# The order of the last two tiles in the expert stage: down products of the second to last tile, and low-part gate and up products of the last

## What is computed

```python
h = jax.nn.silu(jnp.einsum('nd,edf->nef', t, w_gate)) * jnp.einsum('nd,edf->nef', t, w_up)
h = h * gate[:, :, None].astype(h.dtype)
return jnp.einsum('nef,efd->nd', h, w_down).reshape(B, T, D)
...
x = _layernorm(DEEPNORM_ALPHA * x + _moe(x, ...), ln2_g, ln2_b)
```

## Time and profile before

| | |
|---|---|
| time, median of 3 runs | 1675.98 us (1675.69 to 1679.21) |
| profiled execution, its own time | 1673.25 us |
| its span, first to last instruction | 1671.6 us |
| mean granted clock of PE | 0.972 |
| PE busy | 1564.2 us (94%) |
| DVE busy | 846.0 us (51%) |
| ACT busy | 663.7 us (40%) |
| POOL busy | 233.2 us (14%) |

### The profile page before, as it was taken

The page is one execution under the profiler, slowest core; times in us unless marked ns, Lnnn a source line. Parts: engine busy times, 40 slices in busy tenths (PEclk is TensorE's granted clock), DMA queues, the critical chain, the costliest instruction groups (busy, mean ns, idle before and its releaser), DMA issues. The chain is left out here.

```text
span 1671.6 us, 25671 instructions
## 1 busy us (share of the span) xinstructions
PE 1564.2 (94%) x9815; PEld 1425.3 (85%) x9815; DVE 846.0 (51%) x1426; ACT 663.7 (40%) x1117; POOL 233.2 (14%) x292
## 2 busy tenths in 40 slices
PE   7999999999999998999999999999997599999980
PEld 7999899889988787899999999999786488888860
DVE  4433463454035654512132232334647799999986
ACT  5422241222245655522121111113112488888866
POOL 1000120013002111130000000000000253333320
PEclk9999999999999999999999999999998699999995
DMA  6111232125211122070344114113433799999736
GB/s 186 41 39 39 76 109 51 39 67 170 79 45 54 63 66 60 30 248 14 139 123 145 43 38 145 38 39 114 141 116 110 269 263 285 325 303 290 193 61 235
DMA packets 154225, 204.34 MB, mean 122 GB/s; under 512 B 14723, under 2 KB 121235, under 8 KB 154104
## 3 DMA queue, kind: packets, MB, share of 16 engines
q1 hardware_dynamic: 135224, 140.82, 26.8%
q0 software_dynamic: 18880, 61.89, 13.1%
HBM read 152.34 MB, written 50.34 MB: 121 GB/s over the span
## 5 line engine op out<-in xcount | busy, mean ns | idle before, releaser
L380 PE MATMUL ps<-xh,slab_hi 128*128 128x384 f32 (+1 forms) x504 | 170.3, 338 | 1.5 <-DVE slab_lo L733 1.5
L380 PE MATMUL ps<-xh,slab_lo 128*128 128x384 f32 (+1 forms) x504 | 165.3, 328 | 0.0
L380 PE MATMUL ps<-xl,slab_hi 128*128 128x384 f32 (+1 forms) x504 | 164.9, 327 | 0.0
L1896 PE MATMUL ps<-xh,slab_lo 128*128 128x384 f32 (+1 forms) x384 | 125.2, 326 | 0.0
L1896 PE MATMUL ps<-xh,slab_hi 128*128 128x384 f32 (+1 forms) x384 | 125.1, 326 | 0.0
L1896 PE MATMUL ps<-xl,slab_hi 128*128 128x384 f32 (+1 forms) x384 | 125.1, 326 | 0.0
L2097 DVE TENSOR_TENSOR gt_sg<-ps,gt_sg 128x384 f32<-128x384 f32 (+1 forms) x48 | 25.7, 536 | 187.3 <-PE ps L1896 187.2
L380 PEld LDWEIGHTS ps<-xh,slab_hi 128*128 128x128 f32 x504 | 95.1, 189 | 11.6 <-issue 9.8
L2866 PE MATMUL ps<-mo_hi_gu,mo_xh 128*128 128x512 f32 x256 | 100.3, 397 | 0.9 <-ACT mo_xh L2969 0.7
L2866 PE MATMUL ps<-mo_hi_gu,mo_xl 128*128 128x512 f32 x256 | 99.0, 391 | 0.0
L2037 ACT ACTIVATE gt_sg<-ps 128x384 f32<-128x384 f32 (+1 forms) x48 | 22.8, 474 | 191.9 <-PE ps L1896 191.9
(11 more groups left out here) (498 smaller groups left out, 4164.5 us busy)
## 6 DMA issues: line engine op xcount, KB each, us to landing
slab_raw<-in_w_in SPq DMA_DIRECT2D x60, 512.0 KB, 4.3
mo_raw_g<-in_w_e_gate SPq DMA_DIRECT2D x16, 1024.0 KB, 8.2
mo_raw_u<-in_w_e_up SPq DMA_DIRECT2D x16, 1024.0 KB, 14.0
mo_raw_d<-in_w_e_down SPq DMA_DIRECT2D x16, 1024.0 KB, 7.2
gt_oh<-oT_hi SPq DMA_DIRECT2D x3, 2176.0 KB, 9.1
gt_ol<-oT_lo SPq DMA_DIRECT2D x3, 2176.0 KB, 14.3
slab_raw<-in_w_branch SPq DMA_DIRECT2D x24, 256.0 KB, 4.8
x_dram<-slab_raw SPq DMA_DIRECT2D x9, 512.0 KB, 5.3
```

What stands on the lines that cost most here:

```text
L380: mm = eng.matmul(out, w[:, b, k, :], x[:, k, t0:t0 + tn], start=(k == 0 and j == 0), stop=(k == KC - 1 and j == 2), skip_group_check=True)
L1896: last = eng.matmul(out, w[:, s % 2, c, wk, :], x[:, k, t0:t0 + tn], start=(k == 0 and i == 0), stop=(k == ks[-1] and i == 2))
```

## The change

The last iteration's order is changed on three engines; what is computed is the same.

- PE, iteration 30: `down(30)` comes ahead of `in_tails(31)` instead of behind it.
- ACT, behind the loop: `sigmoid(31)` leaves iteration 30. After the copy of half of tile 30's output come the first half of `hi_d` for tile 31, then `sigmoid(31)`, then the second half, then `h_head(31)`. In before it was `h_head(31)` and then both halves.
- DVE, behind the loop: `gate(31)` and `hidden(31)` leave iteration 30. After the copy of the other half of tile 30's output come the first half of `lo_d`, then `gate(31)`, `hidden(31)`, `h_tail(31)`, then the second half, and the semaphore step on `tail_d` after it.
- `last_head_down` and `last_tail_down` take the halves to do as an argument and are called twice; each call loads its table values into registers anew.

```diff
                 transpose_h(i)
-                if i + 1 < NTILE:
+                if i + 2 < NTILE:
                     in_tails(i + 1)
                 if i + 3 < NTILE:
                     transpose_x(i + 3)
                 down(i) if i + 1 < NTILE else last_down()
+                if i + 2 == NTILE:
+                    in_tails(i + 1)
...
-            def last_head_down():
+            def last_head_down(parts):
...
-                for f in range(2):
+                for f in parts:
                     eng.activation(hi_d[:, f, :], from_raw(raw_d, side, 2)[:, f, :], ACT.Copy).then_inc(head_part, 1)
...
-                if i + 1 < NTILE:
+                if i + 2 < NTILE:
                     sigmoid(i + 1)
                 if i + 3 < NTILE:
                     x_heads(i + 3)
             y_copy(NTILE - 2, [0])
+            last_head_down([0])
+            sigmoid(NTILE - 1)
+            last_head_down([1])
             h_head(NTILE - 1)
-            last_head_down()
             y_copy(NTILE - 1, [0])
...
-                for f in range(2):
+                for f in parts:
                     eng.wait_ge(head_part, f + 1)
                     eng.tensor_tensor(lo_d[:, f, :], from_raw(raw_d, side, 2)[:, f, :], f32(hi_d[:, f, :]),
                                       ALU.subtract).then_inc(tail_part, 1)
-                eng.wait_ge(tail_part, 2)
-                eng.sem_inc(tail_d, 1)
...
-                if i + 1 < NTILE:
+                if i + 2 < NTILE:
                     gate(i + 1)
                     hidden(i + 1)
                 if i + 3 < NTILE:
                     x_tails(i + 3)
 
             y_copy(NTILE - 2, 1)
+            last_tail_down([0])
+            gate(NTILE - 1)
+            hidden(NTILE - 1)
             h_tail(NTILE - 1)
-            last_tail_down()
+            last_tail_down([1])
+            eng.wait_ge(tail_part, 2)
+            eng.sem_inc(tail_d, 1)
             y_copy(NTILE - 1, 1)
```

More of the change, by code:

```diff
@@ L3048, in tail_down, with last_tail_down @@
                 eng.tensor_tensor(lo_d[:, :, :], from_raw(raw_d, side, 2), f32(hi_d[:, :, :]), ALU.subtract).then_inc(tail_d, 1)
-            def last_tail_down():
+            def last_tail_down(parts):
                 side = eng.value_load(mo.side_d[NTILE - 1:NTILE, 0:1], min_val=0, max_val=RDN - 1)
-                for f in range(2):
+                for f in parts:
                     eng.wait_ge(head_part, f + 1)
```

## The result

| | median | lowest to highest | runs |
|---|---|---|---|
| before | 1675.91 us | 1673.20 to 1679.56 | 20 |
| changed | 1680.03 us | 1676.15 to 1683.92 | 20 |

The ratio is 1.0022, with a 95% interval of 1.0015 to 1.0029: the change makes the kernel slower, by the medians by 4.1 us, by the interval by 2.5 to 4.9 us. The profiled execution of the changed kernel took a span of 1676.5 us against 1671.6.

A forecast was written before the change was run, and what follows sets the result against it. TensorE bounds most of the kernel (busy 94%); the edit touches some 12 us near the end. Path +2.45 us plus clock +1.7 gives +4.1, on the median 1675.98 us making 1680.1, range 1676.8 to 1683.5.

The forecast's parts named there:

- Step 1: TensorE, tile 30: down(30) still waits for mo_hl, starts at 1620.55 as before, new idle of about 2.3 us, no cost.
- Step 2: TensorE, tile 31: in_tails(31) moves onto the path, starting 1623.42, taking 2.09 us, done at 1625.5 instead of 1620.15.
- Step 3: ACT, DVE and PE, tile 31: everything behind in_tails(31) shifts; last_down waits for mo_hl until 1629.2 against 1626.36, +2.85 us.
- Step 4: last_down and POOL's last add: 0.13 us shorter products and 0.27 us of slack come back, leaving +2.45 us.
- Step 5: TensorE's clock in the two new idles: one fall more than in before, +1.7 us, bounds 0 and 3.4 us.
- rival of two falls: TensorE's clock: both new idles cost a fall, +2.45 + 3.4 = +5.9 us, 1681.9 us; chance 0.17.
- No further fall: TensorE's clock holds in the new idles, or before already pays for one fall: +2.45, 1678.4 us; chance 0.33.
- Not slower: Ahead of last_down: the wait for mo_hi_d held the end and its 2.56 us come back; chance 0.04, including only slightly slower.
- stall: New chain near the end: a register or code stall in a place held covered costs about 1 us, 1681.1; chance 0.06.

The follow-up runs named there:

- the changed one with the gate first: Changed kernel, idles filled with unread products, VectorE running gate(31) and hidden(31) ahead of the first half of the low down weights: ratio 1.0008 [0.9997, 1.0019].
- the filled kernel: Changed kernel with matrix products that nobody reads put into its new idles on TensorE: ratio 1.0008 [0.9996, 1.0019] to the kernel before.

## Why the prediction was right

**Step 1** held: down(30) started 0.06 us behind mo_hl. The idle was 3.0 us, not 2.3, as mo_hl came 2.92 us behind the start of mo_hh instead of 2.16. An idle of DVE of some 1.5 us, put down to issue, decides it. In the changed kernel it stands behind mo_hl of tile 29:

```profile
1611.83 2.29 DVE L3046 TENSOR_TENSOR mo_lo_gu<-mo_raw_g,mo_hi_gu 128x2048 fp32r<-128x2048 f32 x1 [1.57 <-issue]
```

In before it stands one tile earlier (1.54 us, ahead of 1602.33), and DVE has caught up by tile 30: it waits 0.83 us for mo_hi_d there. Of the nine profiles that keep tail_down(30) ahead of h_tail(30) in DVE's list, not counting the one with the new order in every tile, the five with the idle behind tile 29 have 2.84 to 2.97 us, the four with it a tile earlier 2.16 or 2.17. Both kinds turn up in kernels with and without the change (2.93 in before with its idle filled, 2.16 in the changed one with the gate first). But both profiles of before are of the one kind and both of the changed kernel of the other, so that up to 0.8 us of the difference in time comes from this can't be ruled out.

**Step 2** was wrong in what it says, that in_tails(31) moves onto the path, but the number doesn't rest on it. Its 2.09 us aren't a term of the sum: step 3 has the gate begin when mo_lo_d's first half is written (1626.9), a chain from ACT's copy of y that goes round the products. So it is in the trace, where the products' sigmoid was done 0.75 us before the gate began, and with the products back under their cover last_down started no earlier behind down(30) at all. They are on the path with the old order on ACT and DVE, as the run of TensorE's part alone has it.

**Step 3** held. From the start of ACT's copy of y to last_down the forecast has 1629.25 - 1623.22 = 6.03 us; both the changed and the filled kernel show 6.03, where before has 1626.36 - 1623.22 = 3.14. ACT started mo_hi_d 1.33 us behind y's copy (1624.16 to 1625.49), the gate began 1.14 behind L3058, hidden 0.46 behind that. DVE's detour cost the gate its 1.0 us; taking it out brought 0.5 at last_down and 0.25 in D, as mo_hh(31) was held elsewhere then.

**Step 4** held: last_down took 3.03 us at full clock (3.02 forecast), POOL began 0.74 behind the copy (1635.50 to 1636.24), and the slack of 0.27 was used up. Sum at full clock: 2.50 us against 2.45.

**Step 5** came out right in size and not in its parts, which is luck. I took one fall more than before, at 1.7 us. The changed kernel had two in both profiles, one behind each new idle, at 1.27 and 1.48 us. And before, which I took to have none, has one in some executions: it lengthened last_down from 3.15 to 4.59 us, and D by 1.16, since POOL's slack of 0.27 us swallowed the rest. The net in the medians is 4.1 - 2.5 = 1.6 us, by subtraction; how often each kernel falls wasn't measured. My rival of two falls, 1681.9, described the parts better: D grew by 5.27 us between the first two profiles, where the rival's sum has 5.9 and mine 4.1. It missed the median, 1680.03, as I charged each fall with 1.7 us and before with none.

What step 5 took from the Trainium skill (TensorE: Matmul & The Clock Gate, What's actually happening), that the same kernel meets the gate differently from run to run, the two profiles of before show: 2.56 us of idle each, D 10.82 and 11.98.

**The rivals.** "No further fall" is what the filled kernel shows (+2.5 us in D). "Not slower" failed where I put it: the wait for mo_hi_d did go, and mo_hl took its place. No stall beyond the 1.33 us that I had counted for ACT fell on the chain. That the new order on ACT and DVE alone costs as much as the whole change was not in my text: the run of that part alone shows that, given their order, the low-part products could have stayed covered, and that this would have won nothing.

## What to carry to other kernels

Before moving work out from under a wait, ask what the wait is for and who covers it: here eight products filled the time in which another engine prepared the next operand, and putting them behind it bought nothing and opened two idles. Undo each engine's part of a reorder alone, since here either part cost as much as both. In a tail of short bursts the clock is a term of its own, here 2.77 of the 5.27 us that D grew by in the first profiles and by subtraction 1.6 of 4.1 us in the medians, and filling the idles with products that nobody reads separates it from the waits in one run. A term that a forecast names and doesn't add up, like the low-part products here, isn't confirmed by a sum that comes out right: only undoing that part showed that it was off the path.

## What was not expected of the hardware

- The clock falls after idles that don't look long. The same 2.56 us idle ahead of last_down kept it at 1.00 in one execution of before and was followed by 3.3 us at 0.50 in the other. A fall cost 1.16 to 1.48 us of D here, less than the 1.7 that I took from the earlier trace rows.
- A register load directly behind h_tail leaves DVE idle for up to 1.57 us, and not always: in before the idle is 1.54 us at 1602.33 and none at 1611.26. With the load ahead of h_tail it didn't appear in either of two profiles. Which tile it falls on decides whether mo_hl of tile 30 comes 2.16 or some 2.9 us behind the start of mo_hh. Why it comes and goes is open.
